# Splitting the first chunk's modulated input into two and three token tiles, with two loads moved ahead of the third tile of x

## The reference, cut to what matters

```python
mod = silu(cond) @ w_ada + b_ada            # cond is c for 512 latent tokens, c_ctx for 128 context tokens
h = rmsnorm(x, g_pre_mix) * (1 + scale1) + shift1      # 640 tokens x 1024
... = split(h @ w_in)                       # the first product taken is the attention's v
```

## Time and profile before

| what | value |
|---|---|
| median of 3 runs | 1112.26 us (1112.03 to 1112.38) |
| the profiled execution | 1112.61 us, of it 1110.8 us span |
| TensorE busy | 1095.6 us, 99% of the span |
| VectorE busy | 806.5 us, 73% |
| ScalarE busy | 535.3 us, 48% |
| GpSimd busy | 89.7 us, 8% |
| granted TensorE clock, mean | 0.999 |
| moved by DMA | 140.74 MB, mean 127 GB/s |

### The profile page before, as it was taken

One profiled execution on the slowest core, in us unless ns is written; L12 is line 12 of the kernel. 1 busy time (PEld: TensorE's weight loads), 2 busy tenths in 40 slices (PEclk: granted clock), 3 DMA queues, 4 the chain that ended last, 5 costly groups with the idle time before them and its releaser, 6 DMA issues.

```text
span 1110.8 us, 18581 instructions
## 1 busy us (share of the span) xinstructions
PE 1095.6 (99%) x7105; PEld 1030.0 (93%) x7105; DVE 806.5 (73%) x1430; ACT 535.3 (48%) x1028; POOL 89.7 (8%) x148
## 2 busy tenths in 40 slices
PE   6999999999999999999999999999999999999997
PEld 5799998889999999999999889999999999888886
DVE  5767987679769688886788547999987777633534
ACT  5534453545554345655553258555555555433431
POOL 2042233000000031010000012000000000000002
PEclk9999999999999999999999999999999999999999
DMA  9675663353611203543266344234322322424112
GB/s 373 233 238 142 189 177 111 114 152 106 67 58 46 70 19 106 188 140 123 80 215 214 101 154 163 76 121 147 115 77 89 121 96 76 134 76 171 58 38 95
DMA packets 42775, 140.74 MB, mean 127 GB/s; under 512 B 9376, under 2 KB 10944, under 8 KB 41152
## 3 DMA queue, kind: packets, MB, share of 16 engines
q1 hardware_dynamic: 38752, 131.64, 37.3%
q0 software_dynamic: 3936, 7.92, 2.4%
HBM read 126.89 MB, written 12.60 MB: 126 GB/s over the span
## 4 chain that ended last, share of the span: by engine, by line
PE 94%; DMA 2%; DVE 1%; ACT 1%; SPq 1%; issue 0%; POOLq 0%; POOL 0%; ACTq 0%; DVEq 0%
PE ps L2443 29%; PE ps L2444 29%; PE ps L2445 29%; DMA ada<-in_w_first 2%; PE ps L2761 1%; PE ps L2776 1%; DMA condr_a<-in_cond_rows 1%; PE ps L2735 1%; PE ps L2634 1%; PE ps L2638 1%; PE ps L2636 1%; PE ps L2615 0%; DVE prod_a L2122 0%; ACT xnt L1558 0%; PE ps L2736 0%
## 5 line engine op out<-in xcount | busy, mean ns | idle before, releaser
L2445 PE MATMUL ps<-h_hi,w_lo 128*128 128x320 f32 x880 | 271.9, 309 | 0.0
L2444 PE MATMUL ps<-h_lo,w_hi 128*128 128x320 f32 x688 | 212.6, 309 | 0.0
L2443 PE MATMUL ps<-h_hi,w_hi 128*128 128x320 f32 x624 | 195.5, 313 | 0.0
L2445 PEld LDWEIGHTS ps<-h_hi,w_lo 128*128 128x128 f32 x880 | 165.2, 188 | 0.0
L2443 PE MATMUL ps<-w_hi,h_hi 128*128 128x512 f32 x418 | 164.9, 394 | 0.0
L2444 PE MATMUL ps<-w_lo,h_hi 128*128 128x512 f32 x418 | 162.9, 390 | 0.0
L2445 PE MATMUL ps<-w_hi,h_lo 128*128 128x512 f32 x418 | 162.9, 390 | 0.0
L1725 DVE TENSOR_TENSOR w_lo<-raw,w_hi 128x1024 fp32r<-128x1024 f32 x85 | 102.9, 1222 | 46.2 <-ACT w_hi L1250 45.3
L2444 PEld LDWEIGHTS ps<-h_lo,w_hi 128*128 128x128 f32 x688 | 129.2, 188 | 0.1
L1250 ACT ACTIVATE w_hi<-raw 128x1024 fp32r<-128x1024 f32 x85 | 88.5, 1053 | 64.7 <-PE ps L2445 63.5
L2443 PE MATMUL ps<-h_hi,w_lo 128*128 128x320 f32 x384 | 119.1, 310 | 0.0
(11 more groups left out here) (317 smaller groups left out, 2131.8 us busy)
## 6 DMA issues: line engine op xcount, KB each, us to landing
raw<-in_w_blocks SPq DMA_DIRECT2D x182, 512.0 KB, 3.9
ada<-in_w_first SPq DMA_DIRECT2D x8, 1024.0 KB, 17.9
gdram<-stage SPq DMA_DIRECT2D x8, 640.0 KB, 6.6
gt<-gdram SPq DMA_DIRECT2D x8, 640.0 KB, 5.4
xline<-x SPq DMA_DIRECT2D x5, 512.0 KB, 5.0
x<-xline SPq DMA_DIRECT2D x5, 512.0 KB, 7.9
xt<-in_x_sample SPq DMA_DIRECT2D x4, 512.0 KB, 5.5
vg<-vline POOLq DMA_DIRECT2D x32, 64.0 KB, 3.5
```

The costliest lines, as they stand in the source:

```text
L2443: nc.tensor.matmul(dst, wh, xh, start=first, stop=False, skip_group_check=resumed)
L2444: nc.tensor.matmul(dst, wh, xl, start=False, stop=False, skip_group_check=resumed)
L2445: return nc.tensor.matmul(dst, wl, xh, start=False, stop=last, skip_group_check=resumed)
```

## The change

The list of steps at the start is written anew. Chunk 0's h is made in two parts: token tiles 0 and 1 (256 tokens) as soon as these two are transposed, and tiles 2 to 4 (384 tokens) later. The five steps for x's tiles 2 to 4 come behind the early part and behind the first product of tiles 0 and 1. SyncE loads cols, block 0 of w_first and value block 0 ahead of x's tile 2. The SiLU of the conditions (L1502) comes behind tile 1's square. Transposed tiles use other PSUM banks. The load of condr_a is issued as two halves of 512 KB, once block 2 of w_first (not 3) is there and all tiles are transposed, and its SiLU is two operations. The counts of the semaphores follow.

```diff
-    for step, t in (("xsq", 0), ("xsq", 1), ("xturn", 0), ("xsq", 2), ("xsq", 3), ("xturn", 1), ("xsq", 4),
-                    ("xturn", 2), ("xturn", 3)):
-        plan.append((step, t))
+    plan += [("xsq", 0), ("xsq", 1), ("xturn", 0), ("xturn", 1)]
...
     mif = UNIT_OF[("mif", 0)]
+    split_to(1)
     rows(0)
-    plan.append(("xturn", 4))
+    plan.append(("idle_turns", 6))
     columns(0)
-    plan += [("idle_turns", 12), ("h", 0)]
-    split_to(1)
+    plan += [("idle_turns", 8), ("h", 0, 0), ("xsq", 2), ("hsplit", 0, 0), ("first", 0, 0, 2), ("xturn", 2), ("xsq", 3),
+             ("xturn", 3), ("xsq", 4), ("xturn", 4)]
     rows(1)
-    plan += [("idle_turns", 5), ("hsplit", 0)]
+    plan += [("h", 0, 1), ("hsplit", 0, 1)]
     columns(1)
-    plan += [("h", 1), ("first", 0, 0, 2)]
+    plan.append(("h", 1))
     rows(2)
...
+        def turned_part(step):
+
+            if step[1]:
+                return slice(0, T), step[1] + 2
+            return (slice(0, 2 * P), slice(2 * P, T))[step[2]], step[2] + 1
+
         def turned_x(t, hh):
 
-            return ps[:, (0, 2, 6)[t % 3] + hh, :].rearrange("p (k c) -> p k c", k=4)
+            return ps[:, (0, 2, 6, 2, 6)[t] + hh, :].rearrange("p (k c) -> p k c", k=4)
...
                 if t == 1:
                     sp.dma_start(cst[:, 0:160], a["consts"][:, 0:160]).then_inc(const_in, 16)
-                if t == 2:
                     sp.dma_start(cols[:, :], a["cols"]).then_inc(cols_in, 16)
-            for j in range(KD):
+                    sp.dma_start(ada0[:, 0, :], a["w_first"][0]).then_inc(ada_in[0], 16)
+                    load(0)
+            for j in range(1, KD):
...
             pool.wait_ge(x_tr, 2 * TT)
-            pool.wait_ge(ada_in[3], 16)
-            src = bass.AP(a["cond_rows"].tensor, 0, [[0, P], [D, 2], [1, D]])
-            pool.dma_start(condr_a[:, :, :], src).then_inc(condr_in, 16)
+            pool.wait_ge(ada_in[2], 16)
+            for c in range(2):
+                src = bass.AP(a["cond_rows"].tensor, c * D, [[0, P], [1, D]])
+                pool.dma_start(condr_a[:, c, :], src).then_inc((condr_in, state_in)[c], 16)
...
-                    if t == 3:
+                    if t == 1:
                         act.wait_ge(cols_in, 16)
                         nc.scalar.activation(cond[:, :, 0:2], cols[:, R_C:R_C + 16].rearrange("p (c k) -> p k c", c=2),
                                              ACT.Silu).then_inc(cond_rd, 1)
...
                     k = step[1]
-                    if k < 4:
-                        dve.wait_ge(xt_act, TT - 1)
-                    dve.wait_ge(xt_dve, TT)
+                    early = step == ("h", 0, 0)
+                    dve.wait_ge(xt_act, 1 if early else TT - 1)
+                    dve.wait_ge(xt_dve, 2 if early else TT)
...
                     t = step[1]
                     pe.wait_ge(x_nrm, t + 1)
-                    if t >= 3:
-                        pe.wait_ge(xt_dve, t - 2)
-                    if t == 4:
-                        pe.wait_ge(xt_act, 1)
+                    if t == 2:
+                        pe.wait_ge(dve_drain, drains("V", gid("ada_pair", ("first", 0))))
+                    elif t > 2:
+                        pe.wait_ge(xt_dve, t - 1)
+                        pe.wait_ge(xt_act, t - 2)
```

More of the change, by code:

```diff
@@ L1150, in _ @@
                 if step[0] == "bias0":
-                    pool.wait_ge(h_lod, KD)
+                    pool.wait_ge(h_lod, KD + 1)
                     pool.wait_ge(gemm_done, gid("mifs", 0, 0, 1) + 1)
@@ L1545, in _ @@
                 elif step[0] == "dots_in":
-                    act.wait_ge(condr_in, 16)
-                    nc.scalar.activation(condr_a[:, :, :], condr_a[:, :, :], ACT.Silu).then_inc(condr_rd, 1)
+                    for c in range(2):
+                        act.wait_ge((condr_in, state_in)[c], 16)
+                        nc.scalar.activation(condr_a[:, c, :], condr_a[:, c, :], ACT.Silu).then_inc(condr_rd, 1)
                 elif step[0] == "h" and step[1] > 3:
@@ L1562, in _ @@
                     k = step[1]
-                    act.wait_ge(h_aff, k + 1)
-                    nc.scalar.activation(h_hi[:, k, :], xnt[:, k, :], ACT.Copy).then_inc(h_hid, 1)
+                    sl, done = turned_part(step)
+                    act.wait_ge(h_aff, done)
+                    nc.scalar.activation(h_hi[:, k, sl], xnt[:, k, sl], ACT.Copy).then_inc(h_hid, 1)
                 elif step[0] == "na":
@@ L1732, in ada_block @@
                 if adas_done(b) == 1:
-                    dve.wait_ge(condr_rd, 1)
+                    dve.wait_ge(condr_rd, 2)
                 else:
@@ L2062, in _ @@
                                             ALU.mult).then_inc(x_nrm, 1)
-                    if t == TT - 1:
+                    if t == 1:
                         dve.wait_ge(cols_in, 16)
@@ L2077, in _ @@
                     if BLOCKS[step[1]][0] == UNIT_OF[("br", (1, 1))]:
-                        dve.wait_ge(condr_rd, 2)
+                        dve.wait_ge(condr_rd, 3)
                 elif step[0] == "att_split":
@@ L2121, in _ @@
                     for c in range(2):
+                        dve.wait_ge(condr_rd, c + 1)
                         ins = nc.vector.scalar_tensor_tensor(prod0s[c][:, :], ada0[:, k, m * D:(m + 1) * D], 1.0,
@@ L2137, in _ @@
                     k = step[1]
-                    if k < 4:
-                        dve.wait_ge(xt_act, TT - 1)
-                    dve.wait_ge(xt_dve, TT)
+                    early = step == ("h", 0, 0)
+                    dve.wait_ge(xt_act, 1 if early else TT - 1)
+                    dve.wait_ge(xt_dve, 2 if early else TT)
                     dve.wait_ge(mod_in, k + 1)
                     dve.wait_ge(dve_drain, drains("V", gid("ada_pair", ("first", k))))
-                    for c, sl in ((0, slice(0, LAT)), (1, slice(LAT, T))):
+                    late = (0, slice(2 * P if k == 0 else 0, LAT)), (1, slice(LAT, T))
+                    for c, sl in ((0, slice(0, 2 * P)),) if early else late:
                         ins = nc.vector.tensor_scalar(xnt[:, k, sl], xnt[:, k, sl], mod[:, 0, k, c:c + 1],
@@ L2149, in _ @@
                     k = step[1]
-                    dve.wait_ge(h_hid, k + 1)
-                    nc.vector.tensor_tensor(h_lo[:, k, :], xnt[:, k, :], h_hi[:, k, :].bitcast(F32),
+                    sl, done = turned_part(step)
+                    dve.wait_ge(h_hid, done)
+                    nc.vector.tensor_tensor(h_lo[:, k, sl], xnt[:, k, sl], h_hi[:, k, sl].bitcast(F32),
                                             ALU.subtract).then_inc(h_lod, 1)
@@ L2307, in _ @@
                     dve.wait_ge(ms_rd, 3)
-                    dve.wait_ge(state_in, 16)
+                    dve.wait_ge(state_in, 32)
                 elif step[0] == "ml":
@@ L2506, in group @@
                     pe.wait_ge(act_drain, drains("A", gid("ada_row", which)))
-                    if which[1] == 0:
-                        pe.wait_ge(xt_dve, 3)
-                        pe.wait_ge(xt_act, 2)
+                    if which[1] == 1:
+                        pe.wait_ge(xt_dve, TT)
+                        pe.wait_ge(xt_act, TT - 1)
                     for m in range(2):
@@ L2515, in group @@
                     pe.wait_ge(wm_in, 16)
-                    pe.wait_ge(h_aff, KD - 1)
+                    pe.wait_ge(h_aff, KD)
                     for o in range(2):
@@ L2557, in first_unit @@
                 if k == 0:
-                    pe.wait_ge(xt_dve, TT)
-                    pe.wait_ge(xt_act, TT - 1)
+                    pe.wait_ge(xt_dve, TT if t0 else 1)
+                    if t0:
+                        pe.wait_ge(xt_act, TT - 1)
                 n = FIRST_ADA
@@ L2575, in first_unit @@
                     block_ready(BLOCK_OF[n, k // 2])
-                pe.wait_ge(h_lod, k + 1)
+                pe.wait_ge(h_lod, k + 2)
                 for t in range(t0, t1):
@@ L2703, in _ @@
                     for _ in range(step[1]):
-                        nc.tensor.transpose(ps[:, 4, 0:P], ident, ident)
+                        nc.tensor.transpose(ps[:, 5, 0:P], ident, ident)
                 elif step[0] == "use":
```

6 lines of the change are left out of this document (3 added, 3 removed).

## The result

The changed kernel takes 1123.22 us in the median of six executions, against 1112.39 us for the kernel before beside it: 1.0091 of it, 95% interval 1.0081 to 1.0101. It is slower, as forecast, but by 10.8 us where 6.0 was forecast; that lies outside the range. The six executions spread over 1120.27 to 1124.18 us, while those of the kernel before agree within 1.0 us. The execution profiled here is the shortest, 1120.27 us.

What follows compares the result with a forecast made beforehand. The prediction took TensorE's one long stream of products as the bound: 6.5 us later start less 0.5 us given back makes 6.0 us on 1112.61, 1118.6, less 0.35 for the median: 1118.3 us. Range 1117.0 to 1121.5 us.

Steps and rivals of the forecast that it cites:

- The bound: Whole program: one stream of TensorE products, busy 99% of the span; only its start and a 0.5 us wait can matter.
- the mark: Start of chunk 0's product with tiles 2 to 4, at 22.50 us before; forecast 29.0, late by 6.5 us.
- Loads: SyncE's loads: w_first's block 0 lands at 10.0 us, 3.7 earlier, value block 0 at 11.2; nothing moves from block 1 on.
- Rival 2: Loads at the start: w_first's block 0 and value block 0 do not come forward; 1122.1 us, chance 0.05.
- Up to the first product, and tile 2: Early part of chunk 0: product of tiles 0 and 1 starts at 14.95 us, tile 2's transposes at 16.5.
- Tiles 3 and 4, the step that decides: ScalarE's order: each square stands behind the previous tile's copy; 4.2 us per tile, TensorE waits 3.2 us twice.
- Dots: VectorE's dot products: their 2.0 us wait for the conditions goes, giving TensorE back 0.5 us in the gates' product.
- Sum without the clock: Whole kernel at full clock: 6.5 - 0.5 = 6.0 us later, 1118.3 us; chance 0.52.
- TensorE's clock: Half rate in and behind TensorE's two new waits: put at nothing in the forecast, 2.0 to 3.0 us otherwise.
- the rival: TensorE's clock falls in the two waits: 2.0 us more, 1120.3, up to 1121.3 us; chance 0.33.

Runs made afterwards that it cites:

- run 2: The changed kernel with 23 idle transposes put into each of TensorE's two waits, before tile 3's and tile 4's transposes: 1118.40 us, ratio 1.0056.
- Run 3: The changed kernel with the squares of x's tiles 3 and 4 moved ahead of the first product and of tile 2's copy: 1113.75 us, ratio 1.0012.
- run 7: The kernel before with the conditions' load in halves, chunk 0's split and first product ahead of columns(1), five idle transposes dropped: 1111.16 us, ratio 0.9988.
- run 8: The changed kernel measured a third time, to catch one of its longer executions: 1123.41 us, ratio 1.0092.
- run 4: The kernel before with only the conditions' load in two halves, behind block 2 of w_first, and SiLU in two operations: 1111.64 us, ratio 0.9993.
- run 6: The changed kernel with 23 idle transposes in only the second of TensorE's two waits: 1119.14 us, ratio 1.0058.
- run 5: The kernel before with only SyncE's loads moved (cols, block 0 of w_first, value block 0 ahead of x's tile 2): 1117.47 us, ratio 1.0039.
- run 1: The changed kernel measured again, with no edit: 1120.12 us, ratio 1.0070.

## Why the prediction was wrong

*The bound* was read rightly. In runs 2, 3, 7 and 8 the shift of the mark, or of rows(3), less what the gates' product gives back, is the shift of the profiled time within 0.3 us. In run 2, for example, the mark is 7.1 us late, 0.8 come back, and the profiled execution is 6.4 us longer than that of the kernel before.

*Loads.* Block 0 of w_first was forecast for 10.0 and landed 7.3 us after its issue at 2.57, at 9.9; value block 0 for 11.2, landed 8.1 after 3.05, at 11.15. Right. Rival 2 falls.

*Up to the first product, and tile 2.* Forecast 14.95 and 16.5 for the start of the product and of tile 2's transposes, measured 15.33 and 16.82. The 0.4 us at the product come from adarow: rows(0) now ran in TensorE's slow start (1.42 us, against 1.07) and adarow waited for it until 12.60. I had put rows(0) at its later, faster duration. In the profile of run 2 it took 1.94 us and the product started at 15.81, 0.9 us late.

*Tiles 3 and 4, the step that decides.* Forecast rounds of 4.2 us and waits of 3.2 us; measured rounds of 4.0 and 4.1 us from transposes to transposes, and waits of 2.97 and 3.04. Run 3 took away just this order, and the loss fell to 1.4 us. Shown.

*Dots.* Forecast 0.5 us given back. The mechanism was right: the wait in the gates' product is gone in the changed kernel and in run 4. The size was too small: from its start to the `mifc` product it is 6.22 us in the changed kernel (59.01 to 65.23) and 6.23 in run 4, against 7.04, which is 0.8 us. I had taken the wait as the row gives it.

*Sum without the clock.* Forecast 6.0 us later, 1118.3 us; run 2, the same kernel with its clock held, measured 1118.40 us. That it agrees to 0.1 us is partly luck: the mark was 7.1 us late and not 6.5, 0.8 us came back and not 0.5, and the profiled execution was 6.4 us longer, not 6.0.

*TensorE's clock: the step that failed.* The prediction said "I take nothing for the forecast, since 3.2 us is nearer to the short gap than to 7.56, and keep the rest as a rival". The term was put at nothing; against run 2, the profiles show it at 1.75 us in the short execution and 5.0 us in the long one. Both the choice and the size of the rival were wrong. First, the choice: the distance between two lengths of gap was no scale for this, since what stands around a gap counted too. One wait of 3 us left the clock alone (run 6), two with 1 us of work between them brought it down in all three profiles of the changed kernel, and 4.2 us at once did so too (run 5). The rule of the Trainium skill ("TensorE: Matmul & The Clock Gate", Part 1, on the clock gate) that half rate is the default after idleness was the better guide, and the trace now agrees: 0.51 at 25 to 29 us. Second, the size: I priced the rival at 2.0 to 3.0 us by letting the clock return after 2.6 us of work, as at the start of the program. In the short execution it took some 4 us from tile 4's transposes, at a cost of 1.75 us, which is close to the rival's price; in the long one 11.5 us, at a cost of 5.0. Of the 14 executions of the changed kernel seven took 1119.7 to 1120.8 us and seven 1122.6 to 1124.2. Four of the six behind the result were long ones, and that put the median outside the range; the four of run 1 would have put it inside, so whether the range held was a matter of which executions were caught. The range should have taken the recovery's length as unknown, since one instance at the start was all that showed it.

What stays open is why the clock comes back after 4 us of work in one execution and after 11.5 in another of the same program. The three profiles of the changed kernel do differ ahead of it. The slow start lasts longer from one to the next (rows(0) takes 1.42, 1.78 and 1.94 us in the result's profile, run 1's and run 8's), and the clock falls 0.2, 0.5 and 0.9 us behind the last transpose of tile 3. The last of the three is the long one. Three profiles don't show that this is the cause.

## What to carry to other kernels

Where one list sets the order for several in-order engines, a step that only makes work ready (here the squares) belongs ahead of any step whose part on the same engine waits for another engine; read the list once per engine before trusting it. Price a new wait on TensorE twice: as the time it waits, and as a stretch behind it at half clock, whose length varies between executions; if the wait cannot be removed, idle transposes in it are cheap. Loads brought forward push others back: before moving them, look for the gap that this opens on TensorE and for work to fill it. A wait's row can also understate what it costs (0.45 against 0.8 us here): compare distances between starts.

## What the runs showed of the hardware that was not expected

At the start of the program the first transposes are slow (421 ns) with the granted clock given as 1.00; later in the changed kernel the same 421 ns stand beside a granted clock of 0.50. The column is thus no proof of full rate in the first microseconds; durations are.

At half clock the three kinds of work slow down by about the same factor, 1.8 to 1.9: a group of eight transposes from 1.09 to 1.97 us, rows(1) from 1.07 to 1.93, and the distance between the fp32r products of 512 columns from 0.23 to 0.43. So a stretch at half clock costs nearly the double of whatever stands in it.

The clock stayed at half rate from 27.45 to 37 us in run 8 although TensorE had work for all of that time but 0.56 us, and without a pause from 29.93 us on. Working without a pause does not bring it back within a few microseconds in every execution.
